# Attention heads placed among the query projections, output projection by pairs of heads, and waits at the layer seams moved

## What is computed

```
x = x + gla_mixer(rmsnorm(x), ...)              # layer 1: gated linear attention
x = x + conv_ffn(rmsnorm(x), ...)               # first MLP, d_ff 2816, 3-tap convolution
x = x + attn_mixer(rmsnorm(x), ...)             # layer 2: attention
x = x + conv_ffn(rmsnorm(x), ...)               # second MLP
x = second_block(x, c, ...)                     # layer 3: convolution and RWKV branches
```

```
q, k, v = split(h @ w_qkv)
q = rope(rmsnorm(q, q_norm)); k = rope(rmsnorm(k, k_norm))
s = q @ k^T * 128 ** -0.5;  p = softmax(s);  o = p @ v
return o @ w_out
```

## Time and profile before

| | |
|---|---|
| median of three runs | 1169.71 us |
| the profiled execution's own time | 1162.0 us |
| its span, first to last instruction | 1160.2 us |
| TensorE busy | 1084.0 us (93%) |
| VectorE busy | 811.3 us (70%) |
| ScalarE busy | 659.6 us (57%) |
| mean granted TensorE clock | 0.984 of full speed |

### The profile page before, as it was taken

How to read it: one execution, slowest core, us unless ns; L and a number is a source line. 1 busy time by engine, 2 the same in 40 slices (tenths; PEclk the granted TensorE clock), 3 DMA queues, 4 the chain that set the end, 5 groups by cost and what they waited for, 6 DMA issues and landing times.

```text
span 1160.2 us, 25926 instructions
## 1 busy us (share of the span) xinstructions
PE 1084.0 (93%) x10950; PEld 1013.6 (87%) x10950; DVE 811.3 (70%) x1329; ACT 659.6 (57%) x902; POOL 6.5 (1%) x15
## 2 busy tenths in 40 slices
PE   4999988999999987999999988899999999999997
PEld 3999888898989865889999988888889888789997
DVE  4963658757576566477776765598898889955573
ACT  5834546555555654456556554665666657666443
POOL 0000000000000000000000000000000000000000
PEclk9999999999999998989999998999999999999999
DMA  7543345676745331236555553433333233124541
GB/s 242 167 158 108 136 155 181 247 264 229 263 160 182 109 110 37 82 118 208 175 180 195 193 155 121 134 112 110 110 111 110 84 101 111 61 71 129 191 135 37
DMA packets 132990, 167.69 MB, mean 145 GB/s; under 512 B 2656, under 2 KB 124512, under 8 KB 131488
## 3 DMA queue, kind: packets, MB, share of 16 engines
q1 hardware_dynamic: 131632, 153.51, 40.7%
q0 software_dynamic: 1264, 12.78, 2.9%
HBM read 164.18 MB, written 2.10 MB: 143 GB/s over the span
## 4 chain that ended last, share of the span: by engine, by line
PE 79%; DVE 12%; ACT 5%; DMA 2%; issue 2%; SPq 0%; DVEq 0%; ACTq 0%
PE bank L312 17%; PE bank L313 15%; PE bank L314 15%; DVE wl L274 2%; PE banks L615 2%; PE banks L619 2%; PE banks L617 2%; PE bank L615 2%; PE bank L617 2%; PE bank L619 2%; DVE hf L2260 1%; ACT wh L269 1%; PE bank L652 1%; PE banks L1081 1%; PE bank L1113 1%
## 5 line engine op out<-in xcount | busy, mean ns | idle before, releaser
L312 PE MATMUL bank<-xh,wh 128*128 128x256 f32 x1376 | 404.8, 294 | 13.3 <-DVE xl L1811 5.9
L313 PE MATMUL bank<-xl,wh 128*128 128x256 f32 x1408 | 400.0, 284 | 0.0
L314 PE MATMUL bank<-xh,wl 128*128 128x256 f32 x1376 | 390.8, 284 | 0.0
L312 PEld LDWEIGHTS bank<-xh,wh 128*128 128x128 f32 x1376 | 265.1, 193 | 24.0 <-issue 13.1
L274 DVE TENSOR_TENSOR wl<-raw,wh 128x2048 fp32r<-128x2048 f32 x97 | 221.5, 2286 | 74.3 <-ACT wh L269 74.2
L313 PEld LDWEIGHTS bank<-xl,wh 128*128 128x128 f32 x1408 | 271.8, 193 | 0.8 <-issue 0.7
L314 PEld LDWEIGHTS bank<-xh,wl 128*128 128x128 f32 x1376 | 265.3, 193 | 0.0
L269 ACT ACTIVATE wh<-raw 128x2048 fp32r<-128x2048 f32 x97 | 184.7, 1907 | 69.0 <-PE bank L619 52.1
L298 DVE TENSOR_TENSOR wl<-raw,wh 128x1024 fp32r<-128x1024 f32 x86 | 103.7, 1218 | 22.9 <-ACT wh L290 22.8
L2260 DVE SCALAR_TENSOR_TENSOR hf<-big,vecs,hf 128x256 f32<-128x256 f32 x240 | 101.4, 478 | 0.0
L290 ACT ACTIVATE wh<-raw 128x1024 fp32r<-128x1024 f32 x86 | 87.6, 1057 | 8.9 <-PE bank L314 5.5
(11 more groups left out here) (390 smaller groups left out, 2219.2 us busy)
## 6 DMA issues: line engine op xcount, KB each, us to landing
raw<-in_ffn_w_up SPq DMA_DIRECT2D x44, 1024.0 KB, 5.1
raw<-in_w_in SPq DMA_DIRECT2D x36, 1024.0 KB, 5.4
raw<-in_ffn_w_down SPq DMA_DIRECT2D x22, 1024.0 KB, 5.0
raw<-in_gla_w_in SPq DMA_DIRECT2D x12, 1024.0 KB, 6.3
big<-in_ada_w POOLq DMA_DIRECT2D x8, 1536.0 KB, 8.7
raw<-in_attn_w_qkv SPq DMA_DIRECT2D x6, 1024.0 KB, 5.0
raw<-in_gla_w_out SPq DMA_DIRECT2D x4, 1024.0 KB, 5.1
raw<-in_attn_w_out SPq DMA_DIRECT2D x4, 1024.0 KB, 6.7
```

The costliest lines, as they stand in the source:

```text
L312: nc.tensor.matmul(ps, wh, xh, start=start, stop=False)
L313: nc.tensor.matmul(ps, wh, xl, start=False, stop=False)
L314: return nc.tensor.matmul(ps, wl, xh, start=False, stop=stop)
```

## The change

TensorE's attention is one list of calls: each head's steps stand between halves of the query products (`half_of`), and the output projection goes by pairs of heads (`out_part(j, pair)`, 12 matmuls each). Groups 2, 3 and 4 share bank 5, all transposed probabilities bank 7, all head outputs bank 6. ScalarE and VectorE get matching lists.

```diff
+        QK_BANK = (3, 4, 5, 5, 5)
@@ gpsimd: first ada load
+            pool.wait_ge(sem("rstd_ready"), 2)
@@ tensor: mlp
-                    pe.wait_ge(sem("hidden_split"), g0 + s + 1 + i)
+                        if k == 0 or last:
+                            pe.wait_ge(sem("hidden_split"), g0 + s + 1 + i + k)
-                if layer == 0:
-                    pe.wait_ge(out_added, 3)
+                pe.wait_ge(out_added, 6 if layer else 3)
@@ tensor: attention
+            early_product(2, N_QKV, bank_of(N_QKV))
+            pe.wait_ge(sem("rstd_ready"), 3)
...
+            half_of(1, 0)
+            qk_sums(0)
+            half_of(1, 1)
+            half_of(2, 0)
+            qk_turns(0)
+            half_of(2, 1)
+            half_of(3, 0)
+            qk_sums(1)
+            half_of(3, 1)
+            qk_turns(1)
+            half_of(4, 0)
+            qk_sums(2)
             attend_scores(0)
             attend_scores(1)
+            half_of(4, 1)
+            qk_turns(2)
+            turn_probs(0)
+            half_of(5, 0)
+            qk_sums(3)
+            attend_out(0)
+            attend_scores(2)
+            turn_probs(1)
+            half_of(5, 1)
+            qk_turns(3)
+            attend_out(1)
+            attend_scores(3)
+            turn_probs(2)
+            out_part(0, 0)
+            qk_sums(4)
+            attend_out(2)
+            attend_scores(4)
+            turn_probs(3)
+            out_part(1, 0)
+            qk_turns(4)
...
+            for j in range(RING):
+                out_part(j, 3)
+            for pair in range(4):
+                out_part(RING, pair)
@@ tensor: layer 3
+                pe.wait_ge(sem("shift_added"), 1)          # ahead of lora
-            whole(N_L3)
+            for k in range(KT):                            # k outside, m inside
+                if k % 2 == 0:
+                    pe.wait_ge(sem("rms_split"), 16 + k // 2 + 1)
+                for m in range(2):
...
@@ scalar
+                    if modulate:
+                        for k in (2 * g, 2 * g + 1):
+                            ins = nc.scalar.activation(XH[:, k, :], HF[:, k, :], ACT.Identity, bias=mod[:, k:k + 1])
+                if modulate:
+                    for k in range(KT):
...
+                        ins = nc.scalar.activation(HF[:, k, :], HF[:, k, :], ACT.Identity, bias=mod[:, k:k + 1])
+                    ins.then_inc(sem("shift_added"), 1)
@@ scalar: mlp, in the loop
+                    hidden_hi(layer, 0, i)
                     split_hi(act, n0 + 4, i)
-                    hidden_hi(g0, 0, i)
@@ scalar: seams (the same for N_QKV + 2 and N_F1 + 2)
+            split_hi(act, N_F0 + 2)
             norm_split(1)
@@ vector: norm, modulated
-                        ch.step(ins)
-                            ins = v.tensor_scalar(HF[:, k, :], HF[:, k, :], mod[:, 24 + k:25 + k], mod[:, k:k + 1],
+                            ins = v.scalar_tensor_tensor(XL[:, k, :], HF[:, k, :], mod[:, k:k + 1],
+                                                         XH[:, k, :].bitcast(F32), ALU.add, ALU.subtract)
@@ vector: mlp, last round
+                for m in range(2):
+                    dve.wait_ge(sem("gate_silu"), g1 + FI + m)
...
+                    v.tensor_tensor(HID[:, m, :], SGT[:, m, :], CV[:, m, :], ALU.mult).then_inc(sem("hidden_ready"), 1)
+                for m in range(2):
+                    dve.wait_ge(sem("hidden_hi"), g1 + FI + m)
+                    v.tensor_tensor(GL[:, m, :], HID[:, m, :], GH[:, m, :].bitcast(F32), ALU.subtract)\
+                        .then_inc(sem("hidden_split"), 1)
+                split_lo(dve, n0 + 3 * FI)
                 split_lo(dve, n0 + 3 * FI + 1)
@@ vector: seams (the same for N_QKV + 2 and N_F1 + 2)
+            lo(N_F0 + 2)
+            norm(1, lambda k: vec(*first_ffn(k)), between=lambda: first_val(N_F0))
```

More of the change, by code:

```diff
@@ L592, in mlp @@
             def mlp(layer, n0, e0):
[L593 removed]
+                g0 = layer * (FI + 1)
                 def ready(k):
@@ L902, in out_part, with mod_turned @@
                                                 skip_group_check=True)
-                if half:
+                if pair == 3:
                     last.then_inc(block_done, 1)
+            def mod_turned():
+                for h in range(2):
+                    rows = P - 64 * h
+                    for q in range(4):
+                        last = nc.tensor.matmul(PS[3][:, 16 * h + q:16 + 8 * h:4],
+                                                ada_rows[h][0:rows, q * P:(q + 1) * P], ident[0:rows, 0:rows:32],
+                                                start=True, stop=True)
+                last.then_inc(sem("mod_summed"), 1)
@@ new lines, in _ @@
+            early_product(2, N_QKV, bank_of(N_QKV))
+            pe.wait_ge(sem("rstd_ready"), 3)
+            for tt in range(2):
+                last = nc.tensor.transpose(PS[3][:, T + tt * P:T + (tt + 1) * P], RS[:, tt * P:(tt + 1) * P], ident)
+            last.then_inc(sem("rstd_turned"), 1)
+            half_of(1, 0)
[6 more added lines that the diff above has]
+            qk_sums(1)
@@ new lines, in _ @@
+            attend_out(3)
+            attend_scores(5)
+            turn_probs(4)
+            out_part(2, 0)
+            out_part(0, 1)
+            attend_out(4)
+            attend_scores(6)
+            turn_probs(5)
+            out_part(1, 1)
+            attend_out(5)
+            attend_scores(7)
+            turn_probs(6)
+            out_part(2, 1)
+            out_part(0, 2)
+            attend_out(6)
+            turn_probs(7)
+            out_part(1, 2)
+            out_part(2, 2)
@@ new lines, in queries_taken, with values_taken @@
+            def queries_taken(e):
+                n = N_QKV + 1 + e
+                act.wait_ge(block_done, n + 1)
+                nc.scalar.activation(QK[:, QK_AT[e]:QK_AT[e] + 2, :],
+                                     PS[bank_of(n)][:, :].rearrange("p (m t) -> p m t", m=2), ACT.Copy)\
+                    .then_inc(evacuated, 1)
+                qk_square(e)
+            def values_taken():
+                n = N_QKV + 1
+                act.wait_ge(block_done, n + 1)
+                act.wait_ge(sem("rstd_columns"), 1)
+                act.wait_ge(evacuated, E_QKV + 1)
+                for tt in range(2):
+                    last = nc.scalar.activation(VA[:, tt, :], PS[bank_of(n)][:, tt * T:(tt + 1) * T], ACT.Identity,
+                                                scale=small[:, 52 + tt:53 + tt])
+                last.then_inc(evacuated, 1)
@@ L2170, in _ @@
             rope(2)
[L2171 to L2179 removed]
+            normalise(1)
+            lo(N_AOUT + 1)
+            qk_norm(3)
+            negated_max(2)
+            out_lo(0)
+            normalise(2)
+            rope(3)
+            negated_max(3)
+            out_lo(1)
+            normalise(3)
+            lo(N_AOUT + 2)
+            qk_norm(4)
+            negated_max(4)
+            out_lo(2)
+            normalise(4)
+            rope(4)
+            for h in range(5, QH):
+                negated_max(h)
+                out_lo(h - 2)
                 normalise(h)
[L2181 to L2182 removed]
             out_lo(QH - 2)
```

354 lines of the change are left out of this document (164 added, 190 removed).

## The result

The changed kernel takes 1136.47 us as the median of four runs (1135.28 to 1137.76) beside 1167.41 for the kernel before in the same comparison: ratio 0.9733, 95% interval 0.9698 to 0.9768, faster. A second comparison gave 1134.62 us and 0.9728 (0.9705 to 0.9751).

The account below looks back on a forecast made before the run. TensorE bounds the kernel; only its waits and low-clock time can go. Gains 5.1 + 1.1 + 12.9 + 3.7 + 3.2 = 26.0 us, less 4 for clock falls, give 22 off the 1169.7 median: 1148 us, range 1138 to 1160.

Parts of the forecast that it names:

- Parts 1 and 2: First MLP's seam: ada loads held back by an added wait, weight splits put ahead of the norm; 5.1 us.
- Part 3: End of the MLPs: last hidden tile copied and split by halves; 1.1 us after the first MLP, 0.3 after the second.
- Part 4: Attention: same TensorE work in another order with fewer waits, 87.4 us instead of 100.3; 12.9 us.
- (a) to (f): Attention: six TensorE waits expected to remain, 1.8, 1.4, 0.3, 1.7, 1.0 and 1.6 us, sum 7.8.
- Parts 5 and 6: Second MLP's start, 3.7 us, and third layer's norm with a shorter chain to the lora product, 2.9 us.
- The deduction for falls: Whole kernel: nine remaining waits, 3/8 followed by low clock at 1.7 us each, 5.7; 4 us taken off the gain.
- (e): Attention: a remaining TensorE wait of 1.0 us at head 5.
- A: Rival: every remaining wait drops the clock, nine at 1.7 us are 15.3 instead of 4; 1159 us, chance 0.15.
- B: Rival: in attention, half of the 12.9 us is lost to heads' hops counted as covered; 1154 us, chance 0.12.
- C: Rival: late ada loads only move their collision to later block loads, losing 5.1 us; 1153 us, chance 0.08.
- D: Rival: weight splits ahead of a head's next hop stay uncovered, 5.9 us a place with a fall; 1177 us, chance 0.06.
- E: Rival: removed waits only covered others behind them, nothing changes; 1166 to 1170 us, chance 0.04.

Follow-up runs that it names:

- the filled kernel: Kernel before plus 22 unread matmuls of constants (5, 7 and 10) fitted into its three long attention waits: 1161.82 us, ratio 0.9973.
- the old layer-3 seam: Changed kernel with layer 3's norm, modulation, low-rank sum and first product order put back as before: 1140.01 us, ratio 0.9793.
- the overfilled one: Kernel before plus 92 unread matmuls of constants in three attention waits, 40 us of filling in 11.5 us of waits: 1187.50 us, ratio 1.0213.

## Why the prediction was right or wrong

**Parts 1 and 2**, right: 5.6 us for 5.1. The added wait alone gives 3.6 (3.75 said), shown by its removal. The waits behind it were 1.45 (1.65 said) and 1.78 (2.8 said): the walk through VectorE and ScalarE was 1 us too long at the second (its own terms add up to 184.1, not 184.4). The splits ahead of the norms are worth 3.3 us at either MLP, by putting them back; TensorE's wait of 2.33 at the third product was most of it, a fall the rest.

**Part 3**, wrong in size: 0.1 for 1.1. The last down product waits 0.73 less (1.06 for 1.79), but the next early product waits 1.22 where it waited 0.57, since VectorE's two weight splits now stand ahead of the residual adds. The step counted the early product's start from before's 377.05, in which a fall of 1.5 us was contained; that fall went from here, so this place by itself gained 1.6 us, and one of 1.5 us came behind the first down product, at the other end of the stage.

**Part 4**, right in sum: 13.3 for 12.9. Of the waits (a) to (f), 7.8 us in the forecast, the trace has 1.40, 1.29, none, 1.22, 0.68 and 1.52, each at its place. They add up to 6.1. The low clock that the prediction put at 5.5 of the old 100.3 us is 4.0 by the filled kernel; its own row, a mean clock of 0.95 over 100.3 us, allows about 5 at most. So TensorE's own work, which it put at 79.7, is 81.1 (the busy time of the new window, at full clock): waits 1.7 too large and work 1.4 too small nearly cancel, and that the stretch came out at 87.2 for 87.4 is partly luck. The third query weight's split ahead of the norm is 3.3 to 4.4 us of the part, the list of heads the other 9 to 10.

**Parts 5 and 6**, right: 4.4 for 3.7, and with the second MLP's end 3.6 for 3.2.

**The deduction for falls**, wrong; this is the failed step of the working. "9 x 3/8 x 1.7 = 5.7", of which 4 us were taken: one of the nine waits was followed by a fall, at 185.4 us, and it cost 1.5 us. The 26.7 us of the stages hold that already (it is what part 3 lost), so all 4.0 of the deduction are in the miss. The price was near (1.5 measured; the stage from the first down product to the next early product takes 187.40 us with that fall and 185.91 without it, in the trace of the old layer-3 seam). Counted over thirteen traces of this study from 60 to 700 us (all but the overfilled one): of 144 waits from 0.65 to 1.6 us none had a fall of the clock in or right behind it, of 38 from 1.6 to 2.6 us 18 had, of 22 longer ones 21. That is a count of a few places seen again and again, not a law. It also tells which factor failed. The nine waits of the forecast (1.65, 2.8, 1.8, 1.4, 1.7, 1.0, 1.6, 1.95 and, from the second hidden tile's 503.3, 2.4; the 1.0 is (e)) would be charged 5.7 us by this count at 1.5 a fall, as the prediction had it. As they came out (1.45, 1.78, 1.40, 1.29, 1.22, 0.68, 1.52, 1.48 and 1.71), the charge is 1.4, as measured. So the 3/8 was not too high for the waits that the prediction expected; the waits came out shorter than the walk said, and seven of nine lie below 1.6 us, where no trace has a fall.

**The conversion to the median**, wrong, and the larger piece. The 22 us were taken off 1169.7, a median of three runs, while the trace that they came from took 1162.0. The gap was not noise around a constant: in the one slower execution that was traced (1170.46) it is made of the same falls, 3.7 us in the first stage and 3.3 in attention, and the second is what the change removes. The median of three was a high draw besides: in the comparison of the result the kernel before had 1167.41, and in later ones 1162.87, 1165.98 and 1164.92, from 11, 11 and 23 runs. Of the miss of 11.5 us, 4.0 is the deduction, 0.7 the parts, 0.3 rounding, and 6.5 that after's median stands 1.2 us above its profiled execution and before's median of three 7.7. From the profiled basis and without the deduction the same working gives 1136.0.

**The rivals.** A (every remaining wait drops the clock) is refuted: one of nine. The Trainium skill's page "TensorE: Matmul & The Clock Gate", section "A second HAM failure mode: psum-queue depth-cycling", tells of a kernel whose short idles between groups of matmuls make the clock go down and up again. The old attention, with waits of 2.9 to 5.1 us, does so (10.2 us of low clock), and the new one, with 0.7 to 1.5, does not. B lost nothing: the heads' hops are covered. C is out: beside the late ada loads the weight blocks land after 5.0 to 5.1 us. D did not come: in the attention section TensorE waits 6.1 us in all, 1.52 at the longest, where D wanted a whole split of 4.2 us uncovered at five places. E, that nothing changes, is out by the result. Of the signs that the prediction named, the first ada load (163.97), the third product without a wait and the 85 to 90 us of attention (87.2) came as said, and two waits smaller, the down product's (1.78 for 2 to 3) and the first square sum's (1.40 for 1.8). The range was too narrow at its lower end for one reason: its bounds moved the parts and the falls, and none moved the basis.

## What to carry to other kernels

Give a forecast on the basis of the execution that the trace shows, and treat the distance to the median as an unknown of its own, above all when the change removes waits that a fall of the clock can follow. Charge falls by the length of the waits that remain, from counts of waits of that length, and give the charge a range: here an error of 0.4 us in the mean length of nine waits decides between 5.7 us and 1.4. On this chain through three in-order queues, moving a weight split from behind the norm to ahead of it was worth 3 to 4 us a seam: walk the queues to the end and look at which split stands ahead of the step that ends last.

## What the hardware showed that was not expected

The clock can fall without a wait. In five traces (the kernel before's second among them) it fell at 33 to 34 us for 6.8 us, after TensorE had been busy for 18 us without a pause, and the first stage was 3.6 to 3.9 us longer; the same code in seven other traces had no such fall. The two sorts differ ahead of it too: where it came, the first sums took 5.85 to 6.16 us, where it didn't, 5.14 to 5.34 (the changed kernel's are below, the kernel before's second ones are shown above). So 0.6 to 0.9 of the 3.6 to 3.9 us are the sums'.

```profile
14.92 5.28 PE L562 MATMUL bank<-hf,consts 128*128 128x256 f32 x16 [14.92 <-DMA consts<-in_consts]
```

It is not the landing of the constants: one of the five began at 14.48 us, the earliest of all. Two traces with TensorE busy from 2.4 us on had a shorter one, of 3.4 us. Why it falls there stays open. That the slow stretch at the start differs between runs of one kernel is also told by the Trainium skill, page "TensorE: Matmul & The Clock Gate", section "What's actually happening".

Unread matmuls can be worth time, but only if they fit: 22 of them in attention's waits gave 3 us by the medians, 92 cost 25.
